# Weight sums of a Strassen-Winograd down projection: formed by adding DMAs between DRAM tensors instead of on VectorE

## What is computed

```python
xn = rms_norm(x, norm_mix_g)
q, k, v, hc, gb, gc = _project(xn, w_in)
parts = [_dilated_prompt(qf, kf, vf, w, d, slopes) for w, d in zip(WINDOWS, DILATIONS)]
attn_o = _merge_branches(parts)
conv_o = gb * _short_conv(u_ext, w_conv, t)
...
mix = jnp.concatenate([attn_o.reshape(b, t, D_ATTN).astype(x.dtype), conv_o], axis=-1)
h = x + mix @ w_out
hn = rms_norm(h, norm_ffn_g)
return h + (jax.nn.silu(hn @ w_gate) * (hn @ w_up)) @ w_down
```

## Time and profile before

| | us |
|---|---|
| Median of 3 runs | 1216.79 (1215.94 to 1216.95) |
| The profiled execution, device time | 1217.06 |
| Its span, first to last instruction | 1215.3 |
| PE busy | 1197.9 (99%) |
| PE weight loads busy | 1136.5 (94%) |
| DVE busy | 679.3 (56%) |
| POOL busy | 509.6 (42%) |
| ACT busy | 438.1 (36%) |

### The profile page before, as it was taken

How to read it: one execution, slowest core, us unless ns; L and a number is a source line. 1 busy time by engine, 2 the same in 40 slices (tenths; PEclk the granted TensorE clock), 3 DMA queues, 4 the chain that set the end, 5 groups by cost and what they waited for, 6 DMA issues and landing times.

```text
span 1215.3 us, 22908 instructions
## 1 busy us (share of the span) xinstructions
PE 1197.9 (99%) x9257; PEld 1136.5 (94%) x9257; DVE 679.3 (56%) x1133; ACT 438.1 (36%) x828; POOL 509.6 (42%) x420
## 2 busy tenths in 40 slices
PE   7999999999999999999999999999999999999998
PEld 6998779889877799999999999999999999999998
DVE  6888214414677623479555444454554178756665
ACT  7111120000378711355443343334333443445452
POOL 3436023233144341052788768776878640000020
PEclk9999999999999999999999999999999999999999
DMA  5478676343223151012614342245444995323223
GB/s 214 156 281 262 230 262 235 139 174 103 84 92 111 48 185 65 1 45 69 241 48 170 116 149 96 106 175 218 166 173 163 345 342 203 94 88 96 86 74 108
DMA packets 70393, 182.66 MB, mean 150 GB/s; under 512 B 7376, under 2 KB 24464, under 8 KB 66320
## 3 DMA queue, kind: packets, MB, share of 16 engines
q1 hardware_dynamic: 70144, 180.92, 42.5%
q10 hardware_dynamic: 144, 0.27, 0.1%
HBM read 136.33 MB, written 44.83 MB: 149 GB/s over the span
## 4 chain that ended last, share of the span: by engine, by line
PE 48%; DVE 2%; POOL 1%; issue 1%; DMA 0%; ACT 0%; DVEq 0%; ACTq 0%
PE ps L1577 9%; PE ps L1579 9%; PE ps L1578 9%; PE ps L1626 6%; PE ps L1627 6%; PE ps L1628 6%; PE ps L1601 1%; PE ps L1600 1%; PE ps L1602 1%; POOL w_lo L966 1%; DVE norms L2735 1%; DMA w_stage<-in_w 0%; DVE combo_b L2262 0%; POOL w_stage L1009 0%; DVE w_lo L2663 0%
## 5 line engine op out<-in xcount | busy, mean ns | idle before, releaser
L1118 PE MATMUL ps<-act_hi,w_hi 128*128 128x352 f32 x480 | 157.4, 328 | 8.2 <-DVE act_lo L2267 8.2
L1577 PE MATMUL ps<-combo,w_hi 128*128 128x264 f32 x544 | 154.9, 285 | 1.7 <-DVE evac L2651 1.2
L1120 PE MATMUL ps<-act_hi,w_lo 128*128 128x352 f32 x480 | 154.8, 323 | 0.0
L1119 PE MATMUL ps<-act_lo,w_hi 128*128 128x352 f32 x480 | 154.7, 322 | 0.0
L1579 PE MATMUL ps<-combo,w_lo 128*128 128x264 f32 x544 | 154.5, 284 | 0.0
L1578 PE MATMUL ps<-combo,w_hi 128*128 128x264 f32 x544 | 154.3, 284 | 0.0
L1626 PE MATMUL ps<-hid,w_hi 128*128 128x264 f32 x536 | 152.7, 285 | 0.0
L1627 PE MATMUL ps<-hid,w_hi 128*128 128x264 f32 x536 | 152.4, 284 | 0.0
L1628 PE MATMUL ps<-hid,w_lo 128*128 128x264 f32 x536 | 152.3, 284 | 0.0
L966 POOL TENSOR_TENSOR w_lo<-w_stage,w_hi 128x512 fp32r<-128x512 f32 (+1 forms) x51 | 76.2, 1495 | 106.1 <-ACT w_hi L1704 106.0
L1577 PEld LDWEIGHTS ps<-combo,w_hi 128*128 128x128 f32 x544 | 102.2, 188 | 2.1 <-issue 1.4
(11 more groups left out here) (470 smaller groups left out, 3237.1 us busy)
## 6 DMA issues: line engine op xcount, KB each, us to landing
w_stage<-in_w SPq DMA_DIRECT2D x56, 512.0 KB, 4.1
resid<-in_state_k SPq DMA_DIRECT2D x8, 1792.0 KB, 11.0
norms<-in_w SPq DMA_DIRECT2D x22, 512.0 KB, 4.4
t_d<-norms SPq DMA_DIRECT2D x11, 1024.0 KB, 4.9
h_d<-evac SPq DMA_DIRECT2D x36, 264.0 KB, 2.3
v_buf<-in_state_v SPq DMA_DIRECT2D x9, 1024.0 KB, 7.0
resid<-in_xT SPq DMA_DIRECT2D x16, 528.0 KB, 7.3
late<-h_d SPq DMA_DIRECT2D x6, 1056.0 KB, 12.9
```

What stands on the lines that cost most here:

```text
L1118: pe.matmul(out, hi, rhs_hi, start=first, stop=False)
L1119: pe.matmul(out, hi, rhs_lo, start=False, stop=False)
L1120: return pe.matmul(out, lo, rhs_hi, start=False, stop=last)
L1577: pe.matmul(out, hi[:, wk], x_hi[:, k, tk], start=(k == 0 and first), stop=False, skip_group_check=not first)
```

## The change

The signs in the four sums are chosen so that each is a sum of plain blocks only (P5, P3 and P7 come out negated, which DVE makes good when it adds the products: `MINUS`). Then each sum can be made in DRAM: SP copies a block of w_down into its place in t_d, and POOL issues DMAs that add further blocks there (`accum_op`). The loads, DVE subtractions and stores of before are gone. Each add is cut into parts of at most three k, so that a sum takes four DMAs; there are five such sets, 20 DMAs of 384 (or 256) rows of 2 KB.

- Copies on SP: P5 in attention, behind the loads of group 0; P7 behind weight unit 28; then a wait for the four P5 adds, and the copies of P5's sum to P6 and P4.
- Adds on POOL: P5 one part in each of the four attention groups; P4 (block 1,1) around the last units of the output projection, behind a wait for all four copies; P7 and P4 (block 1,0) in pairs 6 to 12, P6 in pairs 14 to 18 and the second half of pair 14.

```diff
@@ SP
             load_second(0)
             load_pair_values(0)
+            sp.dma_start(sums_blocks("P5"), down_blocks(0, 0)).then_inc(sums_copied, 16)
             sp.wait_ge(job_done, IN_JOBS)
...
             unit(28)
+            sp.dma_start(sums_blocks("P7"), down_blocks(0, 1)).then_inc(sums_copied, 16)
+            sp.wait_ge(sums_added, 16 * 4)
+            for product in ("P6", "P4"):
+                sp.dma_start(sums_blocks(product), sums_blocks("P5")).then_inc(sums_copied, 16)
...
-                if len(done) > 1:
-                    store_sums(done[1])
-                    load_sums(sums[0])
...
-            sp.wait_ge(scratch_out, 16 * (KT + HK))
+            sp.wait_ge(sums_added, 16 * 20)
@@ POOL
+            def add_block(product, x, y, part):
+
+                ks = slice(3 * part, min(3 * part + 3, HK))
+                pool.dma_start(sums_blocks(product)[:, ks, :], down_blocks(x, y)[:, ks, :], accum_op=ALU.add
+                               ).then_inc(sums_added, 16)
+
...
                 spread_reciprocals(b + 4)
+                if g == 0:
+                    pool.wait_ge(sums_copied, 16)
+                add_block("P5", 0, 1, g)
                 spread_reciprocals(b + 5)
...
-            for u in range(OUT0 + 3, FFN0):
-                straight(u)
+            straight(OUT0 + 3)
+            straight(OUT0 + 4)
+            straight(OUT0 + 5)
+            pool.wait_ge(sums_copied, 64)
+            add_block("P4", 1, 1, 0)
+            straight(OUT0 + 6)
+            add_block("P4", 1, 1, 1)
+            straight(OUT0 + 7)
+            add_block("P4", 1, 1, 2)
+            add_block("P4", 1, 1, 3)
...
                 weight_low(a, "A3")
+                part = (a - PAIR_FIRST) // 2 - 1
+                if 0 <= part < 4:
+                    add_block("P7", 1, 1, part)
+                elif part >= 4:
+                    add_block("P6", 1, 1, part - 4)
                 weight_low(a, "P7")
...
+                if part == 0:
+                    pool.wait_ge(sums_added, 16 * 9)
+                if 0 <= part < 4:
+                    add_block("P4", 1, 0, part)
+                elif part == 4:
+                    add_block("P6", 1, 1, 3)
@@ DVE
-                dve.tensor_tensor(s1, a21, a22, ALU.add).then_inc(act_sums, 1)
+                dve.tensor_tensor(s1, a22, a21, ALU.subtract).then_inc(act_sums, 1)
...
-                dve.tensor_tensor(a11, s1, a11, ALU.subtract).then_inc(act_sums, 1)
+                dve.scalar_tensor_tensor(a11, s1, -1.0, a11, ALU.mult, ALU.subtract).then_inc(act_sums, 1)
...
-                dve.tensor_tensor(out, two_banks(2 * m), out, ALU.add).then_inc(down_put, 1)
+                dve.tensor_tensor(out, out, two_banks(2 * m), ALU.subtract if DOWN_PRODUCTS[i] in MINUS else ALU.add
+                                  ).then_inc(down_put, 1)
```

More of the change, by code:

```diff
@@ L222, in build @@
                     w_stage[:, 1, 0:512], w_stage[:, 1, 512:1024]]
-        sums_buf = norm_row[:, 0:2048]
         y_last = place(("a", 4), 4).rearrange("p (k t) -> p k t", k=KT)
@@ L303, in build @@
         h_out = [[sem(f"h_out{h}{i}") for i in range(2)] for h in range(2)]
-        sums_in, scratch_out = sem("sums_in"), sem("scratch_out")
+        sums_copied, sums_added, scratch_out = sem("sums_copied"), sem("sums_added"), sem("scratch_out")
         part_in_a = {n: [sem(f"{n}_in{i}") for i in range(3)] for n in ("a11", "a12", "a21", "a22")}
@@ L348, in build @@
             sem(n) for n in ("t_made", "gate1", "gate2", "up2", "hidden1", "hidden2", "dve_lo"))
-        w_sums, act_sums, down_low, down_put = sem("w_sums"), sem("act_sums"), sem("down_low"), sem("down_put")
+        act_sums, down_low, down_put = sem("act_sums"), sem("down_low"), sem("down_put")
         last_ss = sem("last_ss")
@@ L468, in piece_ready, with down_blocks, sums_blocks @@
             eng.wait_ge(part_in_a[name][k // 4], 16)
+        def down_blocks(x, y):
+            return w[DOWN0 + HK * x:DOWN0 + HK * x + HK].rearrange("k p n -> p k n")[:, :, 512 * y:512 * y + 512]
+        def sums_blocks(product):
+            return t_d.rearrange("k p n -> p k n")[:, :, 512 * W_SUMS[product]:512 * W_SUMS[product] + 512]
         def out_half(product, m):
@@ L694, in store_hidden @@
                              ).then_inc(h_out[h][f % 2], 16)
[L696 to L708, removed]
             def put_away(k):
@@ L764, in _ @@
                 n = a + 2
-                sums, done = DOWN_SUMS[a], DOWN_SUMS.get(a - 2, ())
                 store_hidden(0, a - 1)
                 store_hidden(1, a - 1)
-                if len(done) > 1:
-                    store_sums(done[1])
-                    load_sums(sums[0])
-                if a - 2 == PAIR_FIRST:
-                    store_sums(0)
-                    load_sums(1)
                 load_raw(*(("gate", n) if n < PAIR_END else ("up", n)))
                 load_raw(*(("up", n) if n < PAIR_END else ("gate", n)))
[L776 to L780, removed]
                 if n < PAIR_END:
@@ L788, in _ @@
             load_raw("gate", FT - 1)
-            store_sums(HK - 1)
             sp.wait_ge(sub_done, SUBS * len(PAIRS))
@@ L1069, in _ @@
                 weight_low(a, "P3")
-                for product in ("P7", "P5", "P4", "P3"):
-                    weight_low(a + 1, product)
+                weight_low(a + 1, "P7")
+                weight_low(a + 1, "P5")
+                if part == 0:
[4 more added lines that the diff above has]
+                    add_block("P6", 1, 1, 3)
+                weight_low(a + 1, "P4")
+                weight_low(a + 1, "P3")
                 if a + 2 < PAIR_END:
@@ L1930, in down_highs @@
                 product, n = DOWN_PRODUCTS[i], AT[s]
-                if s == 0:
-                    act.wait_ge(scratch_out, 16 * (KT + HK))
                 act.wait_ge(down_in[n % DOWN_RAWS], 16 * (n // DOWN_RAWS + 1))
@@ L2761, in block_low @@
                 dve.tensor_tensor(which[1], block_f[(2, 1, 0, 2)[n]], f32(which[0]), ALU.subtract).then_inc(dve_lo, 1)
[L2763 to L2781, removed]
             def hidden_sums(k):
@@ L2798, in fourth_sum @@
                 dve.wait_ge(act_sums, BLOCK_SUMS + 3 * HK)
-                dve.tensor_tensor(place(HOME["s1"][k]), place(HOME["a12"][k]), place(HOME["a11"][k]), ALU.subtract
-                                  ).then_inc(act_sums, 1)
+                dve.scalar_tensor_tensor(place(HOME["s1"][k]), place(HOME["a12"][k]), -1.0, place(HOME["a11"][k]), ALU.mult,
+                                         ALU.subtract).then_inc(act_sums, 1)
             def down_lows(s):
@@ L2956, in _ @@
                 b, n = a + 1, a + 2
-                sums = DOWN_SUMS[a]
                 put_sub(a, "p1")
@@ L2961, in _ @@
                 put_sub(a, "p7")
-                if sums and a > PAIR_FIRST:
-                    first_down_sums(sums[0])
                 put_sub(a, "p5")
                 put_sub(a, "p4")
-                if sums and a > PAIR_FIRST:
-                    second_down_sums(sums[0])
                 put_sub(a, "p3")
@@ L2976, in _ @@
                 second_up(b)
-                if len(sums) > 1:
-                    first_down_sums(sums[1])
-                elif n < PAIR_END:
+                if n < PAIR_END:
                     pair_t_sums(n + 1)
@@ L2982, in _ @@
                 first_hidden(b)
[L2983 to L2989, removed]
             for f in range(PAIR_END, FT):
@@ L3127 @@
 BLOCK_SUMS, FIRST_PARTS = 8, 32
-DOWN_SUMS = {4: (0,), 6: (), 8: (1,), 10: (2,), 12: (3, 4), 14: (5, 6), 16: (7, 8), 18: (9, 10)}
 POS, GATE_NO, HI_NO, LO_NO, GATE_AT, SUB_AT = {}, {}, {}, {}, {}, {}
@@ L3186 @@
 W_SUMS = {"P5": 0, "P7": 1, "P4": 2, "P6": 3}
+MINUS = ["P5", "P3", "P7"]
 HOME = {"a11": [("a", i) for i in range(8, 19)],
```

## The result

| | before | changed |
|---|---|---|
| Median, us | 1216.37 (1215.80 to 1216.95) | 1225.99 (1225.64 to 1226.98) |
| Ratio to before | | 1.008 [1.0063, 1.0098] |
| Profiled execution, span, us | 1215.3 | 1223.8 |
| PE busy, us | 1197.9 | 1200.5 |
| DVE busy, us | 679.3 | 639.8 |

The change costs 9.6 us, where 17.4 were forecast. 39.5 us of DVE's work are gone and bring nothing that can be seen in the sum.

A forecast was written before the change was run, and what follows sets the result against it. PE was taken to bound the kernel, busy 1197.9 of 1215.3 us. Median 1216.8 plus 17.4 us of PE standing for late x, minus 0 gain, gave 1234 us, range 1216 to 1248.

The forecast's parts named there:

- What bounds the kernel, and how little is to be gained: Whole kernel: PE busy 1197.9 of 1215.3 us; its waits for other engines from 320 us on total 3.1 us, 0.25%.
- The mechanism: Out-projection: x loads queue behind copies on SP, DVE's first addition is late, PE's job 4 stands 17.4 us.
- the copy's duration: SP's DRAM-to-DRAM copies of 2.88 MB: 13.8 us each if both sides share 417 GB/s, 6.9 at load speed; 13.8 taken.
- nothing more is lost: Out-projection after PE's wait: x blocks come each 1.3 us, DVE needs some 1.3 us a job against PE's 2.93.
- Issued at 426.14 in both kernels: SP's queue: the eight x loads are issued at 426.14 us, before and after the change.
- The gain of 0 in the pair stage: Pair stage, 635 to 943 us: removing DVE sums and transfers gains between 0 and 0.9 us, taken as 0.
- POOL's time for an add: Attention, out-projection and pair stage: 1 to 3 us per adding DMA, bounded by 0.44 and 7.2; cost 0.
- D: POOL's own time for one adding DMA; everything is covered below 4.6 us, taken as 1 to 3 us.
- rival (b): Pair stage: POOL is late at 7.2 us an add, costing some 10 to 25 us, time 1244 to 1259; chance 0.10.
- The three-operand sums on DVE: 1000 to 1200 us: 22 sums get a factor of -1, at most 15 us more of DVE; cost 0.
- (a): Copies ahead of x run at load speed, 6.9 us, deciding point under 7.9; time 1216 to 1217; chance 0.13.
- (c): Fourth P5 add lands late, delaying copies and x; at 446, stall 37 us, time 1254; chance 0.07.

The follow-up runs named there:

- e1: Changed kernel with the wait for the P5 adds and the copies to P6 and P4 moved behind the eight x loads: 1215.88 us, ratio 0.9995.
- e12: e1 unchanged, measured again against the kernel before: 1215.88 us against 1216.65, ratio 0.9994.
- e5: Changed kernel with only the copy to P4 moved behind the x loads, the wait and the copy to P6 staying ahead: 1215.81 us, ratio 0.9997.
- e4: Kernel before plus two copies of 2.88 MB to an unused DRAM tensor just ahead of the x loads, no adding DMAs: 1227.88 us, ratio 1.0094.
- e9: As e3, and also without the fourth P5 add: 1215.68 us, ratio 0.9993.
- e3: Changed kernel with P6 and P4 copied from a w_down block instead of P5's sum, without SP's wait for the adds: 1223.20 us, ratio 1.0056.
- e7: Kernel before with the first two weight loads for the sums issued behind tile 7's gate and up loads: 1215.96 us, ratio 0.9997.
- e6: e1 with both adds of a pair issued one right behind the other in the pair stage: 1239.50 us, ratio 1.019.
- e11: As e6, but every add of the pair stage takes one k instead of three: 1218.07 us, ratio 1.0012.

## Why the prediction was right, and where it was off

*What bounds the kernel, and how little is to be gained: right.* With 39 us of DVE work and 33 transfers gone, the traces show 0.8 us less of PE's waits, and the times of e1 and e12 show no change beyond their intervals. (The 1.62, 1.23 and 0.69 us that I called mean costs are medians.)

*The mechanism: right, and shown.* Copies ahead of the x loads in SP's queue make x late, DVE's addition late and PE's job 4 wait: the waits of the profile after, e1 (moved: gone), e5 (half: gone) and e4 (the copies alone: there).

*The size: the copy's duration was the term that was mis-sized.* I had the choice between 6.9 and 13.8 us and took 13.8, by the argument that read and write share 417 GB/s. Measured are 8.9 us in the changed kernel (324 GB/s), 9.6 in e4, and 307 to 380 GB/s in e9. So the two sides don't share the 417 GB/s of a load; at 324 a copy runs some 22% slower than a load. The Trainium skill's 207 to 214 GB/s for copies between HBM tensors (DMA: Bandwidth & Descriptors, Latency and other measured facts), which I had set beside it, was measured there with 16 KiB a partition; this copy, in rows of 2 KB, does not keep to it. Put into my own sum, 3 × 8.9 + 3.8 gives a backlog done at 441.3 instead of 456, and a wait of some 2.7 us, too little.

*Two terms were missing and made up for part of that.* First, the queue ran empty: I had the two copies follow the first without a gap, but SP issued them only when the add had landed, at 425.4, and their flow began near 427.5, while from 420.4 to 426.8 only 0.52 MB had flowed. The add landed 11.9 us behind its issue, not 10.3; its own price for the queue was sized right (3.9 us, e3 against e9). From 427.5, 2 × 8.9 + 1.9 + 0.5 us lead to 447.7, 5.8 us behind the 441.9 at which PE stops; measured are 7.1, and the rest lies in the first of the two copies, which took 10.7 us from 427.5 to its landing. Second, I had written that nothing more is lost behind the wait, but the lower clock took another 2.0 us here, 2.8 in e4. 7.1 + 2.0 = 9.1 against the 17.4 forecast. The forecast held in part by luck: with the copy sized right my sum gives 2.7 us of wait instead of 17.4, and the missing terms put 6.4 us back.

*"Issued at 426.14 in both kernels": wrong.* SP was held in the issue of a store until 435.7. It made no difference to x: the engines were over 90% busy with the copies from 427 to 447, and x followed them without a gap.

*The gain of 0 in the pair stage: wrong by 0.8 us.* The reason given, that what stands behind in a queue hardly slows what stands ahead, fell with e7: 5.7 us against 4.5. It took only the move of two loads, not the work that is gone.

*POOL's time for an add: right.* 1.15 to 1.46 us against 1 to 3. The four attention adds fit in their gaps (3.42 us are left of 4.81), and PE waits for POOL no more than before. But D was the wrong thing to ask for. The price of an add of this size is that the next one is held until it has landed, some 8.3 us. In the output projection it shows and is covered by the 52 idle us. The first three adds there land 10.5, 8.0 and 9.9 us behind their issue, at 474.2, 482.5 and 492.7, and each next one starts 0.3 us later:

```profile
463.69 1.27 POOL L902 DMA_DIRECT2D t_d<-in_w  x1
...
474.48 1.26 POOL L902 DMA_DIRECT2D t_d<-in_w  x1 [5.84 <-issue]
...
482.83 1.27 POOL L902 DMA_DIRECT2D t_d<-in_w  x1 [3.41 <-issue]
493.03 1.15 POOL L902 DMA_DIRECT2D t_d<-in_w  x1 [8.93 <-issue]
```

In the pair stage the adds stand 13.1 and 27.0 us apart, and so cost nothing; e6 shows what rival (b) would have been: some 23 us, though by this hold and not by POOL's own time for an add.

*The three-operand sums on DVE, the copies' and adds' waits in attention, the wait at 20 adds: right at 0.* No wait of PE between 650 and the end but those of before.

*Of the rivals,* (a) seems near by its own point of decision, a copy under 7.9 us against 8.9. But that point also has the two copies follow without a gap. With their flow starting at 427.5, even 6.9 us a copy leads to 427.5 + 13.8 + 1.9 + 0.5 = 443.7, 1.8 us too late for PE. (b) and (c) did not come: PE waits for POOL 0.5 us as before, and the wait for the adds ended at 425.4.

## What to carry to other kernels

A transfer's price is not in its bytes alone but in who stands behind it in the same queue: ask for each load behind it when it is needed. Here one copy ahead of x fitted into 8 us of cover and cost nothing, two cost 10 us, and the move of three lines gave them back. A wait on a queue's issuing engine leaves the queue empty meanwhile: without it (e3) PE's wait was 3.6 us instead of 7.1, with the same copies ahead of x. Idle time of an in-order engine is a cover only where it lies: 9 us idle in 40 did not hide a gap of 7 us.

## What the runs showed of the hardware that was not expected

- A copy of 2.88 MB between DRAM tensors, in rows of 2 KB, flows at 307 to 380 GB/s alone, against 407 to 423 for a load of x; behind the empty stretch of the changed kernel they were 268 to 371.
- An adding DMA of 0.52 MB beside such a copy cut the flow to 138 to 238 GB/s for some 8 us (e3), with the engines 80 to over 90% busy. The copy beside it landed 6.2 us later, the load behind all three copies 3.9.
- POOL issues an adding DMA of 384 rows in 1.27 us (median), but a second one right behind it only when the first has landed (gaps of 5.7 to 7.2 us in four pairs of e6); with 128 rows two of four went out at once (e11).
- SP's issue itself can stand: 15.3 us for the third copy in a row in e3, 8.45 us for a store of 36 KB behind two copies.
- PE's granted clock fell to half around waits of 3.6 us (e3), 7.1 and 7.7, and was full again 4 to 6 us after PE had work; the loss was 2.0 to 2.8 us on top of the wait. In e6 it fell around waits of 2.8 to 3.3 us too, three times only after PE had work again, and cost 5.8 us in four falls; around waits of 1.1 and 1.7 us it stayed full.
